# Decoder layer in split fp32: cross attention's panel low halves kept in HBM, and three engines' step lists in another order

## What is computed

```python
hn = rms_norm(h, norm1_g[l])
proj = hn @ w_in[l]
y_hg = hgrn2_group(hq, hf, hi, hg, lb_all[l], hg_norm_g[l])      # 4 heads, chunks of 64
y_sw = swa_group(sq, sk, sv, positions, ...)                     # 8 q heads, window 128
h = h + concat([y_hg, y_sw]) @ w_out[l]
hn = rms_norm(h, norm2_g[l])
mn = rms_norm(mem, mem_norm_g[l])
h = h + memory_cross_attention(hn, mn, xa_wq, xa_wkv, xa_q_norm_g, xa_k_norm_g, xa_wo)
hn = rms_norm(h, norm3_g[l])
a = relu(hn @ mlp_up[l])
h = h + (a * a) @ mlp_down[l]
```

## Time and profile before

| what | value |
|---|---|
| median of 3 runs | 2501.66 us (2501.6 to 2503.6) |
| the profiled execution | 2495.6 us, of it 2493.8 us span and 1.8 us around it |
| granted clock of PE, mean | 0.998 |
| busy: PE, DVE, ACT, POOL | 2454.1, 1735.3, 1136.4, 880.0 us |
| transfers | 371.54 MB, mean 149 GB/s |

### The profile page before, as it was taken

The page is one execution under the profiler, slowest core; times in us unless marked ns, Lnnn a source line. Parts: engine busy times, 40 slices in busy tenths (PEclk is TensorE's granted clock), DMA queues, the critical chain, the costliest instruction groups (busy, mean ns, idle before and its releaser), DMA issues.

```text
span 2493.8 us, 39390 instructions
## 1 busy us (share of the span) xinstructions
PE 2454.1 (98%) x14110; PEld 2014.8 (81%) x14110; DVE 1735.3 (70%) x3014; ACT 1136.4 (46%) x2164; POOL 880.0 (35%) x1018
## 2 busy tenths in 40 slices
PE   7999999999999999999999999999999999999999
PEld 5878788888887788788878888788888888888887
DVE  6899788788678474766677767876664545565765
ACT  5575566676666456546653223522232232323231
POOL 1433100000000552564337768476673222222222
PEclk9999999999999999999999999999999999999999
DMA  4442643543532531752343343232348653445664
GB/s 188 169 138 94 210 131 114 204 142 115 206 131 94 199 132 46 254 177 85 106 165 119 131 177 111 92 135 102 123 146 292 201 150 114 141 127 150 209 198 137
DMA packets 189187, 371.54 MB, mean 149 GB/s; under 512 B 14273, under 2 KB 80321, under 8 KB 187073
## 3 DMA queue, kind: packets, MB, share of 16 engines
q1 hardware_dynamic: 183840, 359.51, 43.4%
q10 hardware_dynamic: 5152, 9.51, 1.0%
HBM read 286.71 MB, written 79.89 MB: 147 GB/s over the span
## 4 chain that ended last, share of the span: by engine, by line
PE 64%; DVE 2%; issue 1%; DMA 1%; ACT 1%; POOL 0%; DVEq 0%; ACTq 0%; SPq 0%; POOLq 0%
PE bank L3228 8%; PE bank L3226 8%; PE bank L3230 8%; PE bank L3206 7%; PE bank L3203 7%; PE bank L3202 7%; PE bank L2145 4%; PE bank L2140 4%; PE bank L2141 4%; PE bank L2192 1%; PE bank L2171 1%; PE bank L2182 1%; PE bank L2120 1%; PE bank L3181 0%; PE bank L3186 0%
## 5 line engine op out<-in xcount | busy, mean ns | idle before, releaser
L411 POOL TENSOR_TENSOR wlo<-raw,whi 128x256 fp32r<-128x256 f32 x372 | 312.3, 871 | 942.6 <-ACT whi L1113 520.5
L1506 PE MATMUL bank<-hi,whi 128*128 128x512 f32 x704 | 284.5, 404 | 1.8 <-ACT fg L1076 1.8
L3230 PE MATMUL bank<-hi,wlo 128*128 128x512 f32 x896 | 276.0, 389 | 0.0
L3228 PE MATMUL bank<-lo,whi 128*128 128x512 f32 x896 | 276.0, 389 | 0.0
L3226 PE MATMUL bank<-hi,whi 128*128 128x512 f32 x896 | 276.0, 389 | 0.0
L1509 PE MATMUL bank<-lo,whi 128*128 128x512 f32 x704 | 275.6, 392 | 0.2 <-DVE lo L1257 0.2
L3017 DVE TENSOR_TENSOR lo<-h,hi 128x1024 fp32r<-128x1024 f32 x80 | 124.4, 1554 | 172.9 <-ACT hi L2781 172.9
L2712 POOL TENSOR_TENSOR wlo<-h,whi 128x256 fp32r<-128x256 f32 x160 | 126.8, 815 | 300.0 <-ACT whi L2773 300.0
L2140 PE MATMUL bank<-hi,whi 128*128 128x512 f32 x504 | 202.7, 402 | 1.7 <-DVE h L2033 1.3
L2141 PE MATMUL bank<-lo,whi 128*128 128x512 f32 x504 | 196.8, 390 | 0.0
L3226 PEld LDWEIGHTS bank<-hi,whi 128*128 128x128 f32 x896 | 168.3, 188 | 34.8
(11 more groups left out here) (401 smaller groups left out, 5562.1 us busy)
## 6 DMA issues: line engine op xcount, KB each, us to landing
h<-hidden_scratch SPq DMA_DIRECT2D x96, 512.0 KB, 4.2
raw<-w_mix SPq DMA_DIRECT2D x88, 512.0 KB, 4.3
raw<-w_cross SPq DMA_DIRECT2D x64, 512.0 KB, 3.6
raw<-w_mlp SPq DMA_DIRECT2D x64, 512.0 KB, 4.6
wlo<-mixer_lows_scratch SPq DMA_DIRECT2D x60, 512.0 KB, 3.9
hidden_scratch<-hT SPq DMA_DIRECT2D x116, 256.0 KB, 2.1
h<-w_mlp SPq DMA_DIRECT2D x112, 256.0 KB, 3.0
mixer_lows_scratch<-wlo SPq DMA_DIRECT2D x22, 512.0 KB, 2.9
```

What stands on the lines that cost most here:

```text
L411: last = pool.tensor_tensor(wlo[:, i, cols], raw[:, i, cols], whi[:, i, cols].bitcast(F32), ALU.subtract)
L1506: pe.matmul(out, w, hi[:, k, :], start=k == 0, stop=False)
L3228: pe.matmul(down_bank(i)[:], wh[:, cols], xl[:, i % 2, :], start=False, stop=False)
L3230: last = pe.matmul(down_bank(i)[:], wl[:, cols], xh[:, i % 2, :], start=False, stop=K == KD - 1)
```

## The change

**Low halves.** POOL makes the low halves in cross attention only for the first turn's b = 0 uses, 16 panels (the first of them already in the mixer), and for the MLP's first panel. SP stores each of the 16 to a new tensor in HBM, `cross_lows_scratch` (512 KB each), and loads the low half of the other 48 uses from there into `wlo` (`load_low`). PE's part 2 waits for a load (`lows_moved`) in place of POOL's work where the panel isn't split. SP's raw load waits for the high half alone; the wait for POOL's low half now stands ahead of a store.

```diff
+CROSS_SPLITS = [(0, i) for i, (_, b, _) in enumerate(CROSS_PANELS) if b == 0] + [(CROSS_TURNS - 1, CROSS_PAN)]
...
+            def load_low(turn, i):
+                panel_used(sp, turn, i - 2)
+                if (turn, i) > (0, 1):
+                    lows_moved(sp, turn, i - 2)
+                sp.dma_start(wlo[:, i % 2, :].bitcast(F32), cross_lows_d[CROSS_SOURCE[i % CROSS_PAN]]).then_inc(low_moved[i % 2], 16)
...
                     if i == 1:
+                        if turn:
+                            load_low(turn, 0)
...
+                    if i >= 2 and is_split(turn, i - 2):
+                        low_split(sp, turn, i - 2)
+                        sp.dma_start(cross_lows_d[CROSS_SOURCE[i - 2]],
+                                     wlo[:, i % 2, :].bitcast(F32)).then_inc(low_moved[i % 2], 16)
                     if turn or i > 2:
                         sp.wait_ge(w_hi.sem, w_hi.at(turn, i - 2))
-                        sp.wait_ge(w_lo.sem, w_lo.at(turn, i - 2))
                         sp.dma_start(raw[:, i % 2, :], ...)
+                    if i >= 2 and not is_split(turn, i - 1):
+                        load_low(turn, i - 1)
...
-            for turn in range(TURNS):
-                for i in range(1, CROSS_PAN + 1):
-                    pool.wait_ge(w_hi.sem, w_hi.at(turn, i))
-                    panel_used(pool, turn, i - 2)
-                    split_low(pool, i % 2).then_inc(w_lo.sem, 1)
+            for turn, i in CROSS_SPLITS[1:]:
+                pool.wait_ge(w_hi.sem, w_hi.at(turn, i))
+                panel_used(pool, turn, i - 2)
+                if i > 1:
+                    lows_moved(pool, turn, i - 2)
+                split_low(pool, i % 2).then_inc(w_lo, 1)
...
-                    pe.wait_ge(w_lo.sem, w_lo.at(turn, i))
+                    if is_split(turn, i):
+                        low_split(pe, turn, i)
+                    else:
+                        lows_moved(pe, turn, i)
```

**Lists.** The rows of PE, ACT and DVE for the mixer's four blocks, and of the same three engines for both turns of cross attention, are written in another order; the first row and POOL's list are as before. Every step is there again; a few steps of the first turn's last norm stand in the other turn's row. The end of PE's row for block 3:

```diff
-        "o2.3 c10 L2 m14.2 m15.0 u8 m15.1 m15.2 m16.0 m16.1 m16.2 s3.0 s3.1 n4 u9 s3.2 s3.3 u10 u11 T3 D3 p2 c12 c14 "
-        "o3.0 o3.1 o3.2 o3.3 u12 u13 L3 u14 M0 M1 M2 u15 p3",
+        "o2.3 c10 L2 u8 m14.2 m15.0 m15.1 m15.2 m16.0 m16.1 m16.2 s3.0 s3.1 n4 u9 s3.2 u10 u11 T3 s3.3 D3 p2 c12 c14 "
+        "o3.0 o3.1 o3.2 o3.3 u12 u13 L3 M0 u14 u15 p3 M1 M2",
```

24 lines of the change are left out of this document (17 added, 7 removed), and 226 rows, old and new, of tables (CROSS_ORDERS, ORDERS).

## The result

| what | before | after |
|---|---|---|
| median, 7 runs of each on one chip | 2499.3 us (2496.22 to 2503.6) | 2508.56 us (2507.32 to 2512.44) |
| ratio, 95% interval | | 1.0041 (1.0032 to 1.0051) |
| the profiled execution | 2495.6 us, span 2493.8 | 2507.32 us, span 2505.5 |
| busy: PE, DVE, ACT, POOL | 2454.1, 1735.3, 1136.4, 880.0 us | 2456.6, 1692.8, 1137.7, 716.0 us |
| transfers | 371.54 MB | 405.09 MB |

The account below looks back on a forecast made before the run. PE was taken as the bound nearly everywhere, with time left in block 0 and at block 3's end. Terms -3.0 (block 0), -0.5 (end of block 3), -0.5 (cross attention) gave -4.0, from 2501.66 to 2497.7 us; range 2489.5 to 2504.5.

Parts of the forecast that it names:

- part 2: SP's queue in cross attention: 16 stores and 48 low loads cost 0 us while nothing crowds the queue.
- part 3: The mixer's new lists: 3.0 us gain in block 0, 0 in blocks 1 and 2, 0.5 at block 3's end.
- The next load into that buffer waits for the stores: covered too: SP's queue, cross attention: a store's 2.9 us are hidden by the panel that lies between.
- Whose condition was a condition of POOL's work before: SP's queue: the low load ahead of a raw panel waits for its buffer's use; raw panels issue about 3.5 us earlier.
- Block 0, -3.0: Mixer's block 0: the new list fills 4.06 us of DVE idle pieces, less one join of 1.07 us.
- rival 2: Block 0 comes free whole: PE's 6.9 us idle and three lower-clock stretches, 5.1, go; -12.0, 2489.7 us; chance 0.18.
- rival 1: Lists only shift waits in block 0, POOL's work was hidden anyway; cross attention's 0.5 is left, 2501.2 us; chance 0.18.
- End of block 3, -0.5 with bounds of 1.5: Mixer's last block: 0.5 us gain, bounds of 1.5 either side, the larger of two PE waits, 1.53 and 0.73.
- Cross attention, -0.5: Both turns: 0.5 us gain of a possible 2.2, from raw panels issued earlier at the second turn's start.
- Rival 3: Second turn's start: low loads come late, up to 6.1 us of PE waits plus lost clock, 2507.7 us; chance 0.08.
- two rules weighed: Cross attention: the GpSimd/DVE port lock would make the sum -5.7; the 358 GB/s HBM limit, near -1 us.
- Rival 4: New PE waits in blocks 1 to 3, three of 1.7 us with 1.7 of clock: +6.2, 2507.9 us; chance 0.06.

Follow-up runs that it names:

- e13: Kernel before with low halves in HBM, first store early but behind the raw panel, turn-border low load behind raw, memory's loads at panels 9 and 11: 2496.73 us, 1.0002.
- e6: Kernel before with low halves in HBM, and the second turn's first low load issued behind the raw panel: 2502.48 us, 1.0016.
- e5: Kernel before with low halves in HBM, and the first store issued ahead of the set-up wait and the memory's loads: 2502.27 us, 1.0021.
- e18: e13 with the change's lists of cross attention: 2504.46 us, 1.0025.
- e17: e14 with ACT's split of the second cross panel also ahead of the last attention output, as before: 1.0019, block 3 172.38 us.
- e12: e3 with the split of the first cross panel moved earlier on ACT's list of block 3: 2503.84 us, 1.0015, block 3 177.63 us.
- e15: e8 with POOL making the second turn's first six low halves in place of loading them: 2508.36 us, 1.005.
- e16: e13 with POOL making the second turn's first six low halves in place of loading them: 2498.96 us, 1.0005.
- e10: As e13, but with the memory's two loads together at panel 7, and with the change's lists of cross attention: 2504.94 us, 1.0022.
- e1: Kernel before with the low halves kept in HBM and all lists as before, no queue edit: 2504.82 us, 1.0022.
- e3: Kernel before with the change's lists in the mixer alone, low halves made by POOL: 2500.52 us, 1.0011.
- e8: The whole change with two SP queue edits, first store early and second turn's first low load behind the raw panel: 2507.26 us, 1.0042.
- e11: e8 with residual updates 36 and 37 moved earlier on DVE's list of the first turn: 2506.29 us, 1.0022.
- e14: e3 with the first cross product's three parts again ahead of the last turn and last values product: 1.0016, block 3 176.01 us.
- e2: Kernel before with all the change's lists, mixer and cross attention, low halves still made by POOL: 2515.06 us, 1.0066.

## Why the prediction was wrong, by its own steps

The forecast was -4.0 us, 2497.7, with a range up to 2504.5; measured were 2508.56 us, and +9.3 against a before that stood at 2499.3. Four steps failed: the cover of the stores in part 2, the sum for block 0 in part 3, the bound for the end of block 3, and the lists of cross attention, which had no term.

- **"POOL's low halves are worth nothing by themselves" held**: 164 us left POOL, forecast 167, and e13 equals the kernel before.
- **"The next load into that buffer waits for the stores: covered too" failed.** The 2.9 us of a store were right for the median, 3.0. But the first low half of all stands in its buffer from the mixer on, and its store waits in SP's order for set-up and the memory's loads, and then lands in 8.2 us beside them. There is no panel between that covers it. POOL waited 7.42 us, PE 2.36, with a stretch of lower clock. I also named only loads as waiting for the stores; POOL waits for them as well.
- **"Whose condition was a condition of POOL's work before" is true inside a turn and was the error at its border.** On POOL the condition blocked POOL alone; on SP it blocks the raw panel behind it. "Raw panels are issued about 3.5 us earlier" became 1.2 us later with the low halves alone, at just the place where I had put the gain, and they landed in 7.0 us instead of 4.4. Undoing the order (e6) gave the later stages 4.05 us back. With the change's lists beside it the panel did go out earlier, by 1.8 us (PE itself was held up at product 38), so this error costs nothing in the change itself; the store's does.
- **Block 0, -3.0, had the wrong sign: +1.0** (by the medians over kernels +1.4: 198.28 us with the new lists in nine, 196.89 with the old in eleven, which spread from 195.28 to 198.55). Of the four idle pieces of DVE in the earlier trace rows, 0.93, 1.40 and 0.42 us are gone and the 1.31 is down to 0.62; but 1.76 us opened ahead of the last scores, `c14`, which PE now makes at 259.9 us. What was not asked is what PE then waits for. PE's waits for ACT's turned probabilities (pT) in the block, before:

```profile
PE bank L1658 <- ACT pT L1198: 0.7, 1, 0.7
```

  and in the change:

```profile
PE bank L1668 <- ACT pT L1208: 5.1, 4, 1.8
```

  The windows that answer to the earlier trace rows say it in sum:

```profile
106.00:184.00 78.00, 73.62 (x538) 58.96 (x538) 74.80 (x174) 50.28 (x114) 32.29 (x37) 1.00 0.37 125
184.00:275.00 91.00, 86.08 (x804) 68.61 (x804) 85.92 (x200) 53.17 (x120) 31.11 (x36) 1.00 0.37 126
```

  PE is idle 4.4 + 4.9 = 9.3 us where it was 6.9. The lower clock behind the waits is gone from block 0 (1.00 for 0.96), which hides the size of the miss, for the old lists too ran without it in some executions. In three of their eleven profiles (e5, e13, e18) the clock was 1.00 through block 0, and it took 195.28 to 195.33 us; in eight of the nine with the new lists it was, and it took 198.16 to 198.33. Whole block 0 at full clock, first e13, then the change:

```profile
76.80:272.08 195.28, 187.44 (x1633) 151.67 (x1631) 177.56 (x408) 119.82 (x259) 75.03 (x88) 1.00 0.41 142
```

```profile
76.80:275.06 198.26, 188.96 (x1633) 151.49 (x1633) 179.25 (x413) 119.64 (x259) 72.40 (x84) 1.00 0.41 140
```

  So at equal clock the new lists cost block 0 3.0 us, the size of the gain forecast, with the other sign: 1.5 us more of PE's idle time and 1.5 us more of its busy time, of which the second isn't explained. The six profiles of the old lists with two such stretches in block 0 (196.86 to 197.23 us) are only 1.5 to 2.0 us longer than those at full clock, not 2 x 1.7. That half of rival 2 came true in block 0, its PE half did not, and at block 3 the stretch grew longer; rival 1 had the right mechanism, shifted waits.
- **End of block 3, -0.5 with bounds of 1.5: +4.7.** The wait ahead of the delta did fall, from 1.53 to 0.57 us. The prediction saw that the turns lose their cover and priced this by the largest wait there. Two things were missed, in about equal parts. From `u13` on the stage is 2.4 us longer (13.01 for 10.65): two thirds of a product, 2 x 1.81 = 3.6 us, used to fill the wait for the last values product and now stand behind it, and the split of the second panel moved too, which no step of mine counted; e17 gives this part back. Ahead of `u13` it is 2.3 us longer: the waits ahead of the last two scores grew from 0.6 and 1.2 to 1.5 and 2.6 us, and the half clock there costs 2.8 us for 1.7. No step of mine has these waits. Why the scores come later stays open; e12 only shows that an earlier split of the first cross panel doesn't mend it.
- **Blocks 1 and 2 held** (-0.25, forecast 0), **and so did the MLP** (+0.4).
- **Cross attention, -0.5: the first turn +8.1, the second -2.1.** A gain did come, in the second turn: from its first matmul to the MLP's, PE is idle 1.25 us for 2.24 before; the other 1.1 us are busy time and not explained. (The 2.2 us that the prediction held possible left out the turn's last 8.6 us, where PE was idle 1.3.) The first turn's loss is the store (2.36, with 1.7 of clock) and the lists' wait at product 38 (2.89, with 1.7). The second was in no term: no step followed the lists of cross attention to where DVE's update of the residual frees PE's banks.
- **Rival 3** had the place and the sign, transfers that come late at a turn's start, and its price of +10; its mechanism was wrong. It needed a low load to be the late one, and it put the blame on bytes. In the change PE waited for a store by way of POOL, at the first turn's start and not the second's; that store was slow to land (8.2 us), so a crowd of transfers may have had its part there; this was not separated. At the second turn's start e15 and e16 took six low loads away and changed nothing. A low load that PE waited 2.3 and 2.7 us for is seen only in e10 and e18, in the first turn. Where a raw panel was late (e1), crowding and order acted together, and the order alone was enough to undo it (e6). Of the two rules weighed, the one on bandwidth did not decide: the Trainium skill ("DMA: Bandwidth & Descriptors", Specifications) has a core at about 358 GB/s, and the windows above show 388 to 413 over 15 us; here the measurement decides. **Rival 4** was not seen in blocks 1 and 2, and its place at block 3 was right.

## What to carry to other kernels

When work moves from an engine to transfers, its waits move into the queue that issues them, and block everything behind them there: at a loop's borders list each entry's condition and what stands behind it, for the steady state hides what the borders pay. A wait that an engine no longer has must be followed one step further, to what its partner waits for next, before it is counted as a gain. Work that covers a wait can't be priced by the waits that the profile shows while it is in place: the bound of 1.5 us taken from them met a loss of 4.7, of which the moved cover is 2.4. And where the same code runs with and without a stretch of lower clock, two orders are compared at equal clock, or a loss of 3 us looks like one of 1.

## What was not expected of the hardware

- Three waits of PE in the change, of 2.4 to 2.9 us, had a stretch of lower granted clock at them: 0.50 over 6.8 us at the end of block 3 (2.8 us lost), 0.51 over 3.5 us twice in the first turn (1.7 us lost each). It isn't so with every such wait: in e10 PE waited 2.3 and 2.7 us in the first turn, and the clock stayed at 1.00 (866 to 872 and 1036.8 to 1042 us). With the same steps ahead of it, the stretch at block 3 was 6.8 us long in the change, e3, e8, e11, e14 and e15, and 3.4 in e2 and e17.
- One core moved 388 to 413 GB/s for 15 us. The longest of the change's 48 low loads landed in 7.8 us (median 4.2), the longest of its 16 stores in 8.5 (median 3.0), and with the low halves alone a raw panel at the second turn's start took 7.0 at the median of five instead of 4.4.
- The same code before block 0 took 76.8 to 80.5 us in different executions; the six profiles over 79 us have a stretch of lower clock near 62 us, the others none. So a single profile says little about 3 us of a whole run, while block 1, whose list leaves PE no wait, took 185.71 to 185.73 us in all eleven kernels with the old lists.
